# Query head 4 loaded early, with a ring of six slots for the first 18 gathers

## The chip, the cores and the metric

The kernel runs on one core of one Trainium2 chip. The time is the device time of one execution of the whole program, in microseconds (us); lower is better. The core has five engines with queues of their own (PE the matrix engine, DVE the vector engine, ACT the scalar engine, POOL for gathers and odd jobs, SP for plain transfers), 16 DMA engines that serve all queues, SBUF (on-chip memory, 128 partitions) and PSUM (matmul results, 8 banks). An engine executes its queue in order and waits on semaphores that others increment.

## The reference

One layer for 256 prompt tokens and 8 sample tokens, all float32, width 2048: a gated-linear-attention mixer and a short convolution in parallel, an output projection, and then a PEER block, which is where the change lies. Cut to that block:

```python
q = (ht @ w_query).reshape(T, 8, 2, 128)                   # 8 heads, two halves
s1, s2 = q[:, :, 0] @ sub_keys[0].T, q[:, :, 1] @ sub_keys[1].T   # 128 scores each
v1, i1 = top_k(s1, 16);  v2, i2 = top_k(s2, 16)
cand, cidx = v1[..., None] + v2[..., None, :], i1 * 128 + i2
top, pos = top_k(cand, 16);  idx = cidx[pos];  g = softmax(top)
u = expert_u[idx]                                          # gathered rows of 2048
w = g * gelu(einsum('thkd,td->thk', u, x))
out = einsum('thk,thkd->td', w, expert_v[idx])             # gathered rows again
```

Each token gathers 8 heads x 16 rows from expert_u and as many from expert_v, 8 KB each. The output is the normalised sum of the residual and this block, beside the new states.

## The kernel before, in words

**Stages.** Up to about 941 us the kernel projects: PE multiplies blocks of w_in and w_out, which SP loads into the four `raw` tiles, ACT copies to `w_hi` and DVE subtracts to `w_lo`. `mm_done` counts finished projection blocks and goes on counting through the query blocks: the 16 query blocks are numbered from `B_QRY`, two to a head (one per half), so head h is finished at `B_QRY + 2*h + 2`. Then the PEER block begins and lasts to the end.

**Gathers.** The PEER work is cut into 16 blocks g (8 heads for each of two tiles of 128 tokens) with 16 positions s each. For a position one gather brings 128 rows of expert_u (one for each token of the tile, 1 MB in all) and a later one 128 rows of expert_v. The list `order_of` sets their order: in the first block the U gathers of block 0 alone (gathers 0 to 15), from then on the U gather of block g and the V gather of block g-1 in turn, so that gather 16 is U of block 1, gather 17 is V of block 0 at s = 0, and so on; 16 more serve the sample tokens, 528 in all. POOL issues them in this order (`fetch`, L705), each into a ring slot of 8 KB a partition, and `free_slot` (L691) first waits until the gather that had the slot before was consumed. There are `RING = 8` slots, used as n % 8 (`slot_of`, L303). Two lie over `w_lo`, two over `w_hi`, three over `x_tok` (these wait until `x2_turned` says that PE has read it), one over `act_lo`.

**Consumers.** DVE's `dot` (L1450) multiplies a U gather with the tokens and frees its slot. After the sixteenth, ACT applies Gelu (L1029), DVE multiplies with the softmax weights (`weights_of`, L1476), and ACT makes diagonal matrices `diag` (L1040). The V gathers go half to PE, which adds diag x rows into PSUM (`weigh`, L1868), and half to DVE (`weigh`, L1466). Between these DVE runs the selection for the block after (keys_of, pairs_of, experts_of), which gives the indices `idx_all`.

**Query heads.** SP loads the weights of head h into `wq[h]` (16 KB a partition, 2 MB), which has three places, used as h % 3. Head 0 is computed in pieces around 941 us, heads 1 and 2 right behind it. The others are interleaved with the weighing of V rows, as `QUERIES = {1: (3, 4), 2: (5, 6), 3: (7,)}` says: in loop step b = 1 PE computes heads 3 and 4 in quarters between its V rows, and so on. ACT takes the results out (`query_head`, L974), and PE cannot begin the scores of a half, nor the next head but one half, before ACT has read the PSUM bank. `row_scale((1, 2), 2)` (L1556) turns the sums of squares of token tiles 1 and 2 into scales; it waits for a square root on ACT (L1024). `ROWS` says in which block DVE normalises these tiles (`row_tile`).

**What sets the order.** Each engine's instruction list is written out by hand in one block of code for each engine; the ring is the only place where POOL, DVE, PE and the DMA engines pace each other.

Of the kernel before, what the change touches and what calls it, by code (L numbers as in the profile page):

```python
# [17 lines left out]
F32 = mybir.dt.float32  # L18
# [6 lines left out]
P = 128  # L25
# [7 lines left out]
def hybrid_step(nc, x_prompt, x_sample, state_gla, state_conv, norm1_g, w_in, w_alpha_up, b_alpha,  # L33
                gla_norm_g, conv_w, conv_b, w_out, norm2_g, w_query, sub_keys, expert_u, expert_v,
                norm_f_g, y_prompt, y_sample, gla_prompt, conv_prompt, gla_sample, conv_sample):
    D = x_prompt.shape[2]
    TP, TS = x_prompt.shape[1], x_sample.shape[0]
    T = TP + TS
    KT = D // P
# [5 lines left out]
    PH, TOPK = 8, 16  # L45
# [15 lines left out]
    B_QRY = B_OUT + KT  # L61
# [27 lines left out]
    with ExitStack() as ctx:  # L89
        top = (nc.sbuf_base + 63) // 64 * 64  # L90
        where = [top]

        def sb_at(name, shape, dt, at):
            return nc.alloc_sbuf_tensor_at(name, shape, dt, offset=at)

        def room(nbytes):
            at = where[0]
            where[0] += (nbytes + 31) // 32 * 32
            assert where[0] <= nc.sbuf_usable_end, (where[0], nc.sbuf_usable_end)
            return at  # L100

        def size(shape):
            n = 4
            for s in shape[1:]:
                n *= s
            return n
# [4 lines left out]
        def sem(name):  # L111
            return ctx.enter_context(nc.semaphore(name))
# [19 lines left out]
        mean_b = sb("mean_b", [P, 1])  # L132
        keep = where[0]

        where[0] = (where[0] + 255) // 256 * 256
        at_act = where[0]
        act_hi = sb("act_hi", [P, KT, T], F32R)
        act_lo = sb("act_lo", [P, KT, T], F32R)
        at_raw = where[0]
        raw = [sb(f"raw{s}", [P, KT, P]) for s in range(4)]  # L140
        at_w = where[0]
# [3 lines left out]
        at_qk = room(4 * KT * T)  # L145
# [5 lines left out]
        at_tok = room(4 * 3 * D)  # L151
# [99 lines left out]
        diag_s = [sb(f"diag_s{s}", [P, TS]) for s in range(PH)]  # L251

        RING = 8
        ring_at = ([at_act + 3 * size([P, D])] + [at_w + s * size([P, D]) for s in (2, 3, 0, 1)]
                   + [at_tok + s * size([P, D]) for s in range(3)])
        ring = [sb_at(f"ring{s}", [P, D], F32, at) for s, at in enumerate(ring_at)]
        g_row = sb("g_row", [P, D])
        two = 2 * size([P, D])
        wq_at = (at_qk + size([P, D]), at_raw + two, at_raw)
        wq = [sb_at(f"wq{h}", [P, KT, 2 * P], F32, wq_at[h % 3]) for h in range(PH)]  # L260

        xs_rep = sb_at("xs_rep", [P, D], F32, at_h2T)
        gf_row = sb_at("gf_row", [P, D], F32, at_h2T + size([P, D]))
        y_tok = x2_tok

        S_U, S_V = 10, 12
        ROWS = 4
        QUERIES = {1: (3, 4), 2: (5, 6), 3: (7,)}

        def on_pe(g, s):  # L270

            return s % 2 == 0 if g < N_BLK - 1 else s in (0, 3, 6, 9, 12, 14)
# [12 lines left out]
        order_of = []  # L285
# [14 lines left out]

        diag_free = [done_at[n][1] for n, (kind, _, _, who) in enumerate(order_of) if kind == V_ and who == "pe"]

        slot_of = [n % RING for n in range(len(order_of))]  # L303
        before = [max((z for z in range(max(n - 2 * RING, 0), n) if slot_of[z] == slot_of[n]), default=None)
                  for n in range(len(order_of))]
        nth_in_slot = [slot_of[:n].count(slot_of[n]) for n in range(len(order_of))]
# [28 lines left out]
        mm_done = sem("mm_done")  # L335
# [139 lines left out]
        def _(sp):  # L475
# [63 lines left out]
            def load_query(h):  # L539

                sp.dma_start(wq[h][:], wqry[:, :, 2 * h * P:2 * (h + 1) * P]).then_inc(wq_in[h], 16)
# [3 lines left out]
            load_query(1)  # L545
            sp.wait_ge(lo_done, B_QRY)
            load_query(2)
            for h in range(3, PH):
                sp.wait_ge(mm_done, B_QRY + 2 * (h - 3) + 2)
                load_query(h)  # L550

            sp.wait_ge(mm_done, B_END)
# [18 lines left out]
        def _(pool):  # L571
            g = nc.gpsimd
            n = 0
# [117 lines left out]
            def free_slot(n):  # L691

                if before[n] is None:
                    if slot_of[n] in (5, 6, 7):
                        pool.wait_ge(x2_turned, 12)
                else:
                    who, count = done_at[before[n]]
                    if who == "dot":
                        pool.wait_ge(u_used, count)
                    elif who == "dve":  # L700
                        pool.wait_ge(dve_used, count)
                    else:
                        pool.wait_ge(pe_used, count)
# [26 lines left out]
        def _(act):  # L730
# [243 lines left out]
            def query_head(h):  # L974

                n0 = B_QRY + 2 * h
                query_out(n0)
                query_out(n0 + 1)
                scores_out(n0)
                scores_out(n0 + 1)  # L980
# [38 lines left out]
            scores_out(B_QRY + 1)  # L1019
            query_head(1)  # L1020
            soft_exp(1, P, rstd[:, 0:1])
            query_head(2)
            act.wait_ge(ms_done, 3)
            a.activation(root[:, 1:3], mean_sq[:, 1:3], ACT.Sqrt).then_inc(rt_done, 1)  # L1024
            n_soft = 2
            for b in range(1, N_BLK + 1):
                blk = slice((b - 1) * TOPK, b * TOPK)
# [19 lines left out]
                if b + 1 < N_BLK:  # L1047
                    soft_exp(n_soft, P, rstd[:, (b + 1) // PH:(b + 1) // PH + 1])
                    n_soft += 1
                for h in QUERIES.get(b, ()):  # L1050
                    query_head(h)
# [24 lines left out]
        def _(dve):  # L1076
# [496 lines left out]
            for b in range(N_BLK + 1):  # L1573
                for s in range(TOPK):
                    if b < N_BLK:
                        dot(b, s)
                    if b > 0:
                        if s == 0:
                            weights_of(b - 1)
                            if b == S_U + 1:  # L1580
                                dve.wait_ge(ws_gelu, 1)
                                v.tensor_tensor(w_s[:], w_s[:], g_s[:], ALU.mult).then_inc(ws_ready, 1)
                        if not on_pe(b - 1, s):
                            weigh(b - 1, s)
                    if b == S_U and s % 2:
                        dot_s(s // 2)
                    if b == 0:
                        if s == 2:
                            keys_of(1)
                        if s == 4:  # L1590
                            pairs_of(1)
                        if s == 6:
                            experts_of(1)
                        if s == 12:
                            row_scale((1, 2), 2)
                    elif b + 1 < N_BLK:
                        if s == 1:
                            keys_of(b + 1)
                        if s == 4:
                            pairs_of(b + 1)  # L1600
                        if s == 7:
                            experts_of(b + 1)
                    if b == ROWS and s in (9, 12):
                        if s == 9:
                            dve.wait_ge(mm_done, B_END)
                        row_tile(1 if s == 9 else 2)
                    if b == 7 and s in (9, 11, 13):
                        sample_step(s)
                    if b == 8 and s == 9:
                        sample_own()  # L1610
                    for t, at in ((0, 9), (2, S_V + 1)):
                        if b == at:
                            if s == 2:
                                y_add(t)
                            if s == 6:
                                y_mean_of(t)
                            if s == 9:
                                y_scale(t)
# [15 lines left out]
        def _(pe):  # L1634
# [334 lines left out]
                turn_rows(2, j)  # L1969
            for half in range(2):  # L1970
                rest_scores(half)
            for h in range(1, 3):
                for half in range(2):
                    query(B_QRY + 2 * h + half, every_k)
                for half in range(2):
                    scores(B_QRY + 2 * h + half)
# [3 lines left out]
            for b in range(1, N_BLK + 1):  # L1980
                for s in range(TOPK):
# [14 lines left out]
                    if b == S_V and s % 2:  # L1996
                        weigh_s(s // 2)
                        if s // 2 == PH - 1:
                            pe.wait_ge(pe_used, eaten(VS_, 0, PH - 1))
                            pe.sem_inc(sum_ready, 1)  # L2000
                    for m, h in enumerate(QUERIES.get(b, ())):
                        if s % 2 == 0 and 8 * m <= s < 8 * m + 8:
# [55 lines left out]
```

## Time and profile before

| | |
|---|---|
| median of 3 runs | 2312.95 us (2312.52 to 2313.0) |
| profiled execution | 2313.0 us, of which the span is 2311.3 us |
| TensorE clock granted, mean | 0.87 |
| busy: PE, DVE, POOL, ACT | 1789.2, 1602.8, 945.2, 597.6 us |
| gathers (software queue q0 in all) | 597.80 MB |
| plain loads and stores of SP (q1) | 179.97 MB |
| gather, from issue to landing, median | 14.0 us (U), 13.7 us (V) |
| load of one wq tile, from issue to landing, median | 25.8 us |

The span is what lies between the first and the last instruction; 1.7 us lie around it. A busy share over the whole span mixes two stages. Before 941 us PE is busy without a break and the DMA engines are not; afterwards the DMA engines are busy nearly all the time and no engine is. Tile names stand without their numbers, so `ring` is any slot.

### The profile page before, as it was taken

How to read it: one execution, taken by the hardware profiler on the slowest of the kernel's cores; microseconds unless marked ns; L12 is line 12 of the kernel's file. 1: busy time of each engine (PE TensorE's matmuls, PEld its weight loads, DVE VectorE, ACT ScalarE, POOL GpSimd, SP SyncE). 2: the span in 40 equal slices, each digit the busy share in tenths (PEclk: the TensorE clock that was granted, in tenths of full speed). 3: DMA queues.
4: the chain of work that ended last, by engine and by line, in shares of the span. 5: the costliest groups of instructions: out<-in, count | busy, mean ns of one | idle time of the engine just before them, and what ended most of it. 6: DMA issues, size and time to landing. Idle time of an engine off the chain costs nothing.

```text
span 2311.3 us, 24004 instructions
## 1 busy us (share of the span) xinstructions
PE 1789.2 (77%) x9239; PEld 1274.4 (55%) x9239; DVE 1602.8 (69%) x2035; ACT 597.6 (26%) x897; POOL 945.2 (41%) x736
## 2 busy tenths in 40 slices
PE   8999999999999999957786565666644456655565
PEld 8999999999999999834443222222211122122222
DVE  5544556646555554497787888889788887687766
ACT  5333555545545543410110000001000010010001
POOL 2000110110111101266575656557676665567653
PEclk9999999999999999979997767777677777877768
DMA  9866878887878776699999999999999999999997
GB/s 249 215 188 200 230 229 244 245 246 211 255 211 253 218 228 203 233 419 423 423 427 427 427 427 427 427 427 400 427 427 427 428 426 428 427 417 414 427 427 336
DMA packets 433958, 781.58 MB, mean 338 GB/s; under 512 B 39104, under 2 KB 353368, under 8 KB 365736
## 3 DMA queue, kind: packets, MB, share of 16 engines
q0 software_dynamic: 89424, 597.80, 62.1%
q1 hardware_dynamic: 342800, 179.97, 27.7%
q10 hardware_dynamic: 1624, 2.31, 0.3%
q8 instruction: 73, 1.20, 0.2%
q14 instruction: 37, 0.30, 0.0%
HBM read 756.74 MB, written 23.35 MB: 338 GB/s over the span
## 4 chain that ended last, share of the span: by engine, by line
PE 51%; DMA 31%; DVE 7%; POOL 7%; issue 3%; ACT 1%; DVEq 0%; SPq 0%; POOLq 0%; ACTq 0%
DMA ring<-in_expert_v,idx_all 27%; PE bank L1698 12%; PE bank L1699 12%; PE bank L1700 12%; PE bank L1875 10%; POOL ring L709 7%; DVE ring L1454 3%; DMA ring<-in_expert_u,idx_all 2%; DMA ring<-in_expert_v,idx_s 1%; DVE x_tok L1473 1%; PE bank L1810 1%; PE bank L1854 1%; PE bank L1791 1%; DMA ring<-in_expert_u,idx_s 1%; PE bank L1897 0%
## 5 line engine op out<-in xcount | busy, mean ns | idle before, releaser
L1875 PE MATMUL bank<-ring,diag 128*128 128x512 f32 x1008 | 680.7, 838 | 477.8 <-DMA ring<-in_expert_v,idx_all 392.8
L1875 PEld LDWEIGHTS bank<-ring,diag 128*128 128x128 f32 x1008 | 262.8, 273 | 884.5 <-issue 792.6
L1454 DVE CUSTOM_DVE_ANT_0 ring<-ring,xn_tok 128x2048 f32<-128x2048 f32 x256 | 583.6, 2289 | 220.2 <-DMA ring<-in_expert_u,idx_all 214.7
L1698 PE MATMUL bank<-act_hi,w_hi 128*128 128x264 f32 x2272 | 653.6, 288 | 2.4 <-DVE w_lo L1087 2.4
L1699 PE MATMUL bank<-act_lo,w_hi 128*128 128x264 f32 x2272 | 644.5, 284 | 0.0
L1700 PE MATMUL bank<-act_hi,w_lo 128*128 128x264 f32 x2272 | 644.1, 284 | 0.0
L1087 DVE TENSOR_TENSOR w_lo<-raw,w_hi 128x2048 fp32r<-128x2048 f32 x142 | 325.6, 2293 | 319.0 <-ACT w_hi L740 318.2
L709 POOL DMA_INDIRECT ring<-in_expert_u,idx_all x256 | 434.3, 1696 | 267.6 <-DVE w_all L1454 88.7
L709 POOL DMA_INDIRECT ring<-in_expert_v,idx_all x256 | 377.5, 1475 | 276.2 <-PE bank L1875 207.7
L1698 PEld LDWEIGHTS bank<-act_hi,w_hi 128*128 128x128 f32 x2272 | 428.6, 189 | 21.5 <-issue 18.6
L1699 PEld LDWEIGHTS bank<-act_lo,w_hi 128*128 128x128 f32 x2272 | 429.0, 189 | 1.7 <-issue 1.7
L1700 PEld LDWEIGHTS bank<-act_hi,w_lo 128*128 128x128 f32 x2272 | 426.7, 188 | 0.0
L740 ACT ACTIVATE w_hi<-raw 128x2048 fp32r<-128x2048 f32 x142 | 272.1, 1916 | 423.5 <-PE bank L1700 417.6
L1473 DVE SCALAR_TENSOR_TENSOR x_tok<-ring,w_all,x_tok 128x2048 f32<-128x2048 f32 (+1 forms) x130 | 305.2, 2348 | 31.7 <-DMA ring<-in_expert_v,idx_all 25.8
L663 POOL DMA_DIRECT2D out<-s_ring x64 | 35.0, 546 | 496.0 <-DVE s_ring L1305 496.0
L1029 ACT ACTIVATE w_all<-w_all 128x16 f32<-128x16 f32 x16 | 3.4, 216 | 626.6 <-DVE w_all L1454 626.6
L1854 PE MATMUL bank<-h2T,wq 128*128 128x264 f32 x448 | 103.3, 386 | 0.0
L1854 PEld LDWEIGHTS bank<-h2T,wq 128*128 128x128 f32 x448 | 85.0, 190 | 23.3 <-issue 10.2
L984 ACT ACTIVATE soft<-soft,rstd 128x16 f32<-128x16 f32 x16 | 4.9, 307 | 288.7 <-DVE soft L1397 288.7
L637 POOL DMA_DIRECT2D v_samples<-v_tok x1 | 0.8, 757 | 164.1 <-DVE v_tok L1213 164.1
L1897 PE MATMUL bank<-ring,diag_s 128*8 128x512 f32 x64 | 38.2, 754 | 24.4 <-DMA ring<-in_expert_v,idx_s 24.4
L1040 ACT ACTIVATE diag<-ident,w_all 128x128 f32<-128x128 f32 x127 | 38.8, 388 | 62.0 <-DVE w_all L1479 62.0
(299 smaller groups left out, 1139.5 us busy)
## 6 DMA issues: line engine op xcount, KB each, us to landing
raw<-in_w_in SPq DMA_DIRECT2D x129, 1024.0 KB, 6.7
s_ring<-in_state_gla POOLq DMA_DIRECT2D x64, 256.0 KB, 5.8
out<-s_ring POOLq DMA_DIRECT2D x64, 256.0 KB, 5.8
raw<-in_w_out SPq DMA_DIRECT2D x16, 1024.0 KB, 5.6
wq<-in_w_query SPq DMA_DIRECT2D x8, 2048.0 KB, 25.8
v_row<-v_samples POOLq DMA_DIRECT2D x32, 256.0 KB, 6.1
ring<-in_expert_u,idx_all POOLq DMA_INDIRECT x256, 14.0
ring<-in_expert_v,idx_all POOLq DMA_INDIRECT x256, 13.7
```

Of the source, the lines that this page charges most:

```text
L709: g.indirect_dma_start(ring[slot_of[n]][:], None, table, bass.IndirectOffsetOnAxis(ap=idx, axis=0)).then_inc(ring_in[slot_of[n]], 16)
L740: a.activation(w_hi[n0 % 2][:], raw[s][:], ACT.Copy).then_inc(hi_done, 1)
L1040: a.activation(diag[n_diag % N_DIAG][:], ident[:], ACT.Copy, scale=w_all[:, col:col + 1]).then_inc(diag_ready, 1)
L1087: v.tensor_tensor(w_lo[n0 % 2][:], raw[s][:], w_hi[n0 % 2][:].bitcast(F32), ALU.subtract).then_inc(lo_done, 1)
L1454: v.tensor_tensor_reduce(ring[k][:], ring[k][:], xn_tok[:, b // PH, :], 1.0, 0.0, ALU.mult, ALU.add, w_all[:, b * TOPK + s:b * TOPK + s + ...
L1473: v.scalar_tensor_tensor(out=y_tok[:, t, mine], in0=ring[k][:, mine], scalar=w_all[:, b * TOPK + s:b * TOPK + s + 1], in1=y_tok[:, t, mine ...
L1698: mm(out, hi_, act_hi[:, k, :], start=(k == 0), stop=False)
L1699: mm(out, hi_, act_lo[:, k, :], start=False, stop=False)
L1700: ins = mm(out, lo_, act_hi[:, k, :], start=False, stop=(k == KT - 1))
L1854: ins = mm(out, w[:, k, cols_], h2T[:, k, :], start=(k == 0), stop=(k == KT - 1))
L1875: ins = mm(bank[sum_bank(t) + j][:], diag[nth % N_DIAG][:], ring[k][:, j * 512:(j + 1) * 512], start=first, stop=stop)
L1897: ins = mm(bank[sum_bank(2) + j][0:TS, :], diag_s[s][:], ring[k][:, j * 512:(j + 1) * 512], start=(s == 0), stop=(s == PH - 1))
```

## The change

Six things are edited together.

- The start of `act_hi` is no longer rounded up to 256 bytes. It was at 20480 and is now at 20288, so all that is laid out behind it moves down by 192 bytes, and the ring slots and `raw` tiles now start 64 bytes past a multiple of 256.
- `wq[4]` gets a place of its own over the two `w_hi` tiles, and SP loads it as the fourth, as soon as the last projection is finished (`mm_done >= B_QRY`), before head 3. The waits of heads 5 to 7 are those of the places that they now take over.
- The two ring slots that lie there come last in the list (6 and 7). Gathers 0 to 17 use the first six slots alone, and the first use of slots 6 and 7, gathers 24 and 25, waits for PE to finish head 4 (`mm_done >= B_QRY + 10`).
- PE computes heads 3 and 4 ahead of all weighing, behind heads 1 and 2; ACT takes them out ahead of the Gelu of block 0. Heads 5, 6 and 7 move up to steps 1 and 2.
- The square root for tiles 1 and 2 moves on ACT ahead of head 2, and `row_scale` on DVE from s = 12 to s = 6 of step 0.
- `ROWS` goes from 4 to 3.

```diff
--- before.py
+++ after.py
@@ -132,7 +132,6 @@
         mean_b = sb("mean_b", [P, 1])
         keep = where[0]
 
-        where[0] = (where[0] + 255) // 256 * 256
         at_act = where[0]
         act_hi = sb("act_hi", [P, KT, T], F32R)
         act_lo = sb("act_lo", [P, KT, T], F32R)
@@ -251,21 +250,21 @@
         diag_s = [sb(f"diag_s{s}", [P, TS]) for s in range(PH)]
 
         RING = 8
-        ring_at = ([at_act + 3 * size([P, D])] + [at_w + s * size([P, D]) for s in (2, 3, 0, 1)]
-                   + [at_tok + s * size([P, D]) for s in range(3)])
+        ring_at = ([at_act + 3 * size([P, D]), at_w + 2 * size([P, D]), at_w + 3 * size([P, D])]
+                   + [at_tok + s * size([P, D]) for s in range(3)] + [at_w, at_w + size([P, D])])
         ring = [sb_at(f"ring{s}", [P, D], F32, at) for s, at in enumerate(ring_at)]
         g_row = sb("g_row", [P, D])
         two = 2 * size([P, D])
-        wq_at = (at_qk + size([P, D]), at_raw + two, at_raw)
-        wq = [sb_at(f"wq{h}", [P, KT, 2 * P], F32, wq_at[h % 3]) for h in range(PH)]
+        wq_at = (at_qk + size([P, D]), at_raw + two, at_raw, at_qk + size([P, D]), at_w, at_raw + two, at_raw, at_qk + size([P, D]))
+        wq = [sb_at(f"wq{h}", [P, KT, 2 * P], F32, at) for h, at in enumerate(wq_at)]
 
         xs_rep = sb_at("xs_rep", [P, D], F32, at_h2T)
         gf_row = sb_at("gf_row", [P, D], F32, at_h2T + size([P, D]))
         y_tok = x2_tok
 
         S_U, S_V = 10, 12
-        ROWS = 4
-        QUERIES = {1: (3, 4), 2: (5, 6), 3: (7,)}
+        ROWS = 3
+        QUERIES = {1: (5, 6), 2: (7,)}
 
         def on_pe(g, s):
 
@@ -300,7 +299,8 @@
 
         diag_free = [done_at[n][1] for n, (kind, _, _, who) in enumerate(order_of) if kind == V_ and who == "pe"]
 
-        slot_of = [n % RING for n in range(len(order_of))]
+        FEW = 6
+        slot_of = [n % FEW if n < 3 * FEW else (n - 3 * FEW) % RING for n in range(len(order_of))]
         before = [max((z for z in range(max(n - 2 * RING, 0), n) if slot_of[z] == slot_of[n]), default=None)
                   for n in range(len(order_of))]
         nth_in_slot = [slot_of[:n].count(slot_of[n]) for n in range(len(order_of))]
@@ -545,8 +545,12 @@
             load_query(1)
             sp.wait_ge(lo_done, B_QRY)
             load_query(2)
-            for h in range(3, PH):
-                sp.wait_ge(mm_done, B_QRY + 2 * (h - 3) + 2)
+            sp.wait_ge(mm_done, B_QRY)
+            load_query(4)
+            sp.wait_ge(mm_done, B_QRY + 2)
+            load_query(3)
+            for h in (5, 6, 7):
+                sp.wait_ge(mm_done, B_QRY + 2 * (h - 4) + 2)
                 load_query(h)
 
             sp.wait_ge(mm_done, B_END)
@@ -691,8 +695,10 @@
             def free_slot(n):
 
                 if before[n] is None:
-                    if slot_of[n] in (5, 6, 7):
+                    if slot_of[n] in (3, 4, 5):
                         pool.wait_ge(x2_turned, 12)
+                    if slot_of[n] >= FEW:
+                        pool.wait_ge(mm_done, B_QRY + 10)
                 else:
                     who, count = done_at[before[n]]
                     if who == "dot":
@@ -1019,9 +1025,10 @@
             scores_out(B_QRY + 1)
             query_head(1)
             soft_exp(1, P, rstd[:, 0:1])
-            query_head(2)
             act.wait_ge(ms_done, 3)
             a.activation(root[:, 1:3], mean_sq[:, 1:3], ACT.Sqrt).then_inc(rt_done, 1)
+            for h in (2, 3, 4):
+                query_head(h)
             n_soft = 2
             for b in range(1, N_BLK + 1):
                 blk = slice((b - 1) * TOPK, b * TOPK)
@@ -1591,7 +1598,6 @@
                             pairs_of(1)
                         if s == 6:
                             experts_of(1)
-                        if s == 12:
                             row_scale((1, 2), 2)
                     elif b + 1 < N_BLK:
                         if s == 1:
@@ -1969,7 +1975,7 @@
                 turn_rows(2, j)
             for half in range(2):
                 rest_scores(half)
-            for h in range(1, 3):
+            for h in range(1, 5):
                 for half in range(2):
                     query(B_QRY + 2 * h + half, every_k)
                 for half in range(2):
```

How PE's queue stands behind head 2, before. `wq_202` to `wq_204` are the weights of heads 2 to 4, `keysT` marks the scores of a head, `ring,diag` the weighing of one gather of V rows:

```order
L1854 MATMUL bank<-h2T,wq_202 128x264 x32
L1865 MATMUL bank<-keysT,stage_139 128x128 x2
L1865 MATMUL bank<-keysT,stage_138 128x128 x2
L1875 MATMUL bank<-ring_192,diag_175 128x512 x4
L1854 MATMUL bank<-h2T,wq_203 128x264 x8
L1875 MATMUL bank<-ring_196,diag_176 128x512 x4
L1854 MATMUL bank<-h2T,wq_203 128x264 x8
L1875 MATMUL bank<-ring_192,diag_177 128x512 x4
L1854 MATMUL bank<-h2T,wq_203 128x264 x8
```

And after the change:

```order
L1860 MATMUL bank<-h2T,wq_202 128x264 x32
L1871 MATMUL bank<-keysT,stage_139 128x128 x2
L1871 MATMUL bank<-keysT,stage_138 128x128 x2
L1860 MATMUL bank<-h2T,wq_203 128x264 x32
L1871 MATMUL bank<-keysT,stage_139 128x128 x2
L1871 MATMUL bank<-keysT,stage_138 128x128 x2
L1860 MATMUL bank<-h2T,wq_204 128x264 x32
L1871 MATMUL bank<-keysT,stage_139 128x128 x2
L1871 MATMUL bank<-keysT,stage_138 128x128 x2
L1881 MATMUL bank<-ring_196,diag_175 128x512 x4
L1860 MATMUL bank<-h2T,wq_205 128x264 x8
```

Two whole heads now stand between the scores of head 2 and the first weighing, which reads gather 17.

ACT's queue from the softmax of block 1 to the first diagonal matrices, before. `q_s` and `stage` take out a half head, `sc` its scores, `root` is the square root, `w_all` the Gelu:

```order
L984 ACTIVATE soft<-soft,rstd 128x16 [waits soft_in]
L962 ACTIVATE q_s<-bank 128x8 [waits mm_done]
L964 ACTIVATE stage_139<-bank 128x256
L962 ACTIVATE q_s<-bank 128x8 [waits mm_done]
L964 ACTIVATE stage_138<-bank 128x256
L971 ACTIVATE sc<-bank 128x2x128 [waits sc_mm] x2
L1024 ACT_TABLE_LOAD
L1024 ACTIVATE root<-mean_sq 128x2 [waits ms_done]
L1029 ACT_TABLE_LOAD
L1029 ACTIVATE w_all<-w_all 128x16 [waits u_used]
L1040 ACTIVATE diag_175<-ident,w_all 128x128 [waits w_ready]
```

After the change, the same stretch up to the outputs of head 2:

```order
L990 ACTIVATE soft<-soft,rstd 128x16 [waits soft_in]
L1029 ACT_TABLE_LOAD
L1029 ACTIVATE root<-mean_sq 128x2 [waits ms_done]
L968 ACTIVATE q_s<-bank 128x8 [waits mm_done]
L970 ACTIVATE stage_139<-bank 128x256
L968 ACTIVATE q_s<-bank 128x8 [waits mm_done]
L970 ACTIVATE stage_138<-bank 128x256
L977 ACTIVATE sc<-bank 128x2x128 [waits sc_mm] x2
```

The same five rows of output follow once more for head 3 and once for head 4, of which the last two are shown, and behind them:

```order
L970 ACTIVATE stage_138<-bank 128x256
L977 ACTIVATE sc<-bank 128x2x128 [waits sc_mm] x2
L1036 ACT_TABLE_LOAD
L1036 ACTIVATE w_all<-w_all 128x16 [waits u_used]
L1047 ACTIVATE diag_175<-ident,w_all 128x128 [waits w_ready]
L1047 ACTIVATE diag_176<-ident,w_all 128x128
```

The square root with its wait for DVE (`ms_done`) now stands ahead of head 2, and the Gelu behind the outputs of head 4.

POOL's queue from gather 16 on, before. `ring_191` to `ring_198` are slots 0 to 7, and the semaphore names who must have freed the slot:

```order
L709 DMA ring_191<-in_expert_u,idx_all 128x2048 [waits u_used,retrieved]
L709 DMA ring_192<-in_expert_v,idx_all 128x2048 [waits u_used]
L709 DMA ring_193<-in_expert_u,idx_all 128x2048 [waits u_used]
L709 DMA ring_194<-in_expert_v,idx_all 128x2048 [waits u_used]
L709 DMA ring_195<-in_expert_u,idx_all 128x2048 [waits u_used]
L709 DMA ring_196<-in_expert_v,idx_all 128x2048 [waits u_used]
L709 DMA ring_197<-in_expert_u,idx_all 128x2048 [waits u_used]
L709 DMA ring_198<-in_expert_v,idx_all 128x2048 [waits u_used]
L709 DMA ring_191<-in_expert_u,idx_all 128x2048 [waits u_used]
L709 DMA ring_192<-in_expert_v,idx_all 128x2048 [waits pe_used]
```

After:

```order
L715 DMA ring_195<-in_expert_u,idx_all 128x2048 [waits u_used,retrieved]
L715 DMA ring_196<-in_expert_v,idx_all 128x2048 [waits u_used]
L715 DMA ring_191<-in_expert_u,idx_all 128x2048 [waits u_used]
L715 DMA ring_192<-in_expert_v,idx_all 128x2048 [waits u_used]
L715 DMA ring_193<-in_expert_u,idx_all 128x2048 [waits u_used]
L715 DMA ring_194<-in_expert_v,idx_all 128x2048 [waits u_used]
L715 DMA ring_195<-in_expert_u,idx_all 128x2048 [waits u_used]
L715 DMA ring_196<-in_expert_v,idx_all 128x2048 [waits pe_used]
L715 DMA ring_197<-in_expert_u,idx_all 128x2048 [waits mm_done]
L715 DMA ring_198<-in_expert_v,idx_all 128x2048 [waits mm_done]
L715 DMA ring_191<-in_expert_u,idx_all 128x2048 [waits u_used]
```

The first gather that waits for PE's weighing (`pe_used`) is gather 25 before and gather 23 after, and everything behind it on POOL waits with it.

## Rows read from the trace of the kernel before

**Rows 1.** The page: busy tenths of the DMA engines in 40 slices of the span.
```profile
DMA  9866878887878776699999999999999999999997
```

**Rows 2.** Busy time by stretch, DMA share and GB/s last; the header names the columns.
```profile
core 0: us, PE busy (x) PEld busy (x) DVE busy (x) ACT busy (x) POOL busy (x), PEclk, DMA share, GB/s
...
943.00:959.00 16.00, 16.00 (x144) 16.00 (x143) 9.47 (x41) 8.16 (x20) 0.00 (x0) 1.00 0.01 2
...
1020.00:1030.00 10.00, 4.97 (x6) 2.18 (x7) 9.93 (x16) 3.95 (x10) 6.76 (x4) 0.51 1.02 419
```

**Rows 3.** DMA queues (packets, MB, share of 16 engines), stretch 955 to 1060.
```profile
q0 software_dynamic: 4880, 35.60, 80.3%
q1 hardware_dynamic: 6192, 6.29, 17.2%
```

**Rows 4.** DMA queues, stretch 955 to 1040.
```profile
q0 software_dynamic: 3704, 27.07, 75.5%
q1 hardware_dynamic: 6164, 6.27, 21.2%
```

**Rows 5.** DMA queues, stretch 1110 to 1145.
```profile
q0 software_dynamic: 1775, 12.92, 87.4%
q1 hardware_dynamic: 1775, 1.82, 14.6%
```

**Rows 6.** DMA queues, stretch 1150 to 1200.
```profile
q0 software_dynamic: 2928, 21.33, 101.0%
```

**Rows 7.** DMA queues, stretch 1229 to 1240 (q1 holds gf_row).
```profile
q1 hardware_dynamic: 144, 1.05, 22.6%
```

**Rows 8.** DMA queues, stretch 963 to 964.
```profile
q0 software_dynamic: 12, 0.10, 23.2%
```

**Rows 9.** PE in order of time (start us, us, line, tiles, count, [idle before]).
```profile
966.29 14.41 PE L1854 MATMUL bank<-h2T,wq 128*128 128x264 f32 x64
...
981.78 14.41 PE L1854 MATMUL bank<-h2T,wq 128*128 128x264 f32 x64
996.03 1.42 PE L1865 MATMUL bank<-keysT,stage 128*128 128x128 f32 x8
1025.03 6.10 PE L1875 MATMUL bank<-ring,diag 128*128 128x512 f32 x8 [27.58 <-ACT diag L1040]
...
1034.53 3.60 PE L1875 MATMUL bank<-ring,diag 128*128 128x512 f32 x8
...
1052.24 3.67 PE L1875 MATMUL bank<-ring,diag 128*128 128x512 f32 x8 [2.79 <-DMA ring<-in_expert_v,idx_all]
```

**Rows 10.** ACT in order of time.
```profile
997.48 0.38 ACT L971 ACTIVATE sc<-bank 128x256 f32<-128x256 f32 x1 [0.42 <-PE bank L1865]
997.88 1.28 ACT L1024 ACT_TABLE_LOAD   x1
1015.08 0.20 ACT L1024 ACTIVATE root<-mean_sq 128x2 f32<-128x2 f32 x1 [15.91 <-DVE mean_sq L1563]
...
1022.27 0.22 ACT L1029 ACTIVATE w_all<-w_all 128x16 f32<-128x16 f32 x1 [5.69 <-DVE w_all L1454]
...
1024.57 2.45 ACT L1040 ACTIVATE diag<-ident,w_all 128x128 f32<-128x128 f32 x8 [2.08 <-DVE w_all L1479]
```

**Rows 11.** DVE in order of time.
```profile
1001.24 2.29 DVE L1454 CUSTOM_DVE_ANT_0 ring<-ring,xn_tok 128x2048 f32<-128x2048 f32 x1
...
1014.51 0.33 DVE L1561 TENSOR_REDUCE ssq<-x_ss 128x1 f32<-128x4 f32 x2
...
1015.51 2.29 DVE L1454 CUSTOM_DVE_ANT_0 ring<-ring,xn_tok 128x2048 f32<-128x2048 f32 x1
...
1024.37 0.17 DVE L1479 TENSOR_TENSOR w_all<-w_all,g_all 128x16 f32<-128x16 f32 x1
```

**Rows 12.** POOL in order of time.
```profile
959.06 1.04 POOL L709 DMA_INDIRECT ring<-in_expert_u,idx_all  x1 [82.33 <-DVE idx_all L1440]
...
1031.40 0.94 POOL L709 DMA_INDIRECT ring<-in_expert_v,idx_all  x1 [3.73 <-PE bank L1875]
```


## The prediction

> **What bounds the kernel now.** I read the page's strip of DMA shares first [rows 1]: from slice 18 (about 980 us) on it stands at 9 to the end, where before it wanders between 6 and 8. The stretches confirm it. In 943 to 959 us, while PE is busy all 16 us, the DMA engines are idle (share 0.01) [rows 2]; from 960 us they are full, 419 GB/s in 1020 to 1030, although the clock of PE and the work of the others vary. In a clean stretch gathers alone move 21.33 MB in 50 us, 0.427 MB/us [rows 6]. The 528 gathers are 528 x 1.0486 = 554 MB, which at that rate is 1297 us, the length of the stage. So the end of the program is set by two numbers alone: how many bytes are left at some point near 1060 us, and whether the DMA engines ever run dry after 960 us. I price every edit in these. The second limit to keep in view is DVE, busy 9.93 of 10 us at 1020 to 1030 [rows 2]: in the first block it paces the gathers, and the loads of wq fill what it leaves free.
>
> **The early load of head 4: a gain.** Before, up to 1060 us, three wq tiles pass in the crowded stage (6.29 MB on q1) beside 35.60 MB of gathers [rows 3], and two more follow. Afterwards wq[4] goes as soon as the last projection is done, at about 941 us, into the idle stretch; wq[3] still waits for head 0. What a wq tile costs in the crowd: in 1110 to 1145 us gathers move 12.92 MB where 35 x 0.427 = 14.94 were possible, so 1.82 MB of wq displace 2.02 MB [rows 5], a factor 1.11. A tile of 2.10 MB costs 2.33 MB or 5.4 us. The edit gives 5.4 us if nothing runs dry. Both ends: 4.9 us (2.10 MB at 0.427) and 5.4; I take 5.4.
>
> **Heads 3 and 4 ahead of the weighing, with the root ahead of head 2: a stall.** I follow the chain in order of time.
> - DVE ends the selection of block 1 at 1001.24, where its next dot starts, and row_scale now comes right there. From its first row to the root on ACT it took 1015.08 - 1014.51 = 0.57 us [rows 10, 11]. So the root is at 1001.8, and only then does ACT take out head 2, whose matmuls ended before 996.03 [rows 9]. PE waits until then. Two outputs of 0.4 us and the scores later, head 3 starts at about 1003.3.
> - A head takes PE 981.78 - 966.29 = 15.5 us [rows 9] at the full clock. Heads 3 and 4 end, with their scores, near 1003.3 + 31.0 = 1034.3; PE has idled 6 us and may begin at 1.2 GHz, for which I add 0.7 us (bounds 0 and 3): 1035.0.
> - ACT then ends the last score copy, 1.8 us from the start of the scores as in 996.03 to 997.86 [rows 9, 10], of which 0.4 to 0.6 lie behind the 1035.0: 1035.5. The table load is now on the path, 1.28 us [rows 10] (before it was over long before the Gelu at 1022.27). Gelu 0.22, DVE's multiplication 0.2 [rows 11] and the first diagonal 0.46 (1024.57 to 1025.03): PE weighs gather 17 from 1037.7, where before it did from 1025.03.
> - That weighing took 6.1 us at the low clock in 1025.03, and 3.6 to 3.7 in 1034.53 and, after 2.79 us of idle, in 1052.24 [rows 9]. PE now comes warm from head 4, so I take 3.8 (bounds 3.6 and 6.1): slot 5 is free at 1041.5.
>
> The Trainium skill bears on one term. ACT's table load shows 1.28 us, and on the row no gap behind it. The Trainium skill (ScalarE: Activation LUTs, "What ACT_TABLE_LOAD costs") counts a drain on top and gives 2.66 us for a switch. By the page as an estimate the stall is 1.4 us longer and the forecast that much later; no row here has work queued ahead of such a load and waited for behind it, so the sum keeps the row.
>
> **What the stall does to the DMA engines.** With six slots, gather 23 takes the slot of gather 17, the first V row of PE; before it was gather 25 that waited for it (POOL at 1031.40, right behind the weighing that began at 1025.03) [rows 9, 12]. Gathers 0 to 22 wait for dots alone, the last of them (block 1, s = 0) ended at 1024.37 [rows 11] ahead of the wait for the Gelu. So the DMA engines get 23 gathers, 24.12 MB, and four wq tiles, 8.39 MB, together 32.5 MB, and then nothing until gather 23. Before they moved 27.07 + 6.27 = 33.3 MB up to 1040 [rows 4]. At 0.42 MB/us the supply is out 2 us earlier, at 1038. Gather 23 is issued at 1041.7. From issue to first bytes took from 959.06 to between 963 and 964, where q0 shows its first 12 packets [rows 8, 12], so 4.5 us: bytes flow again at 1046.2. By the slow ends (cold PE in head 3 and in the weighing, +2.3 each) it is 1050.8; by the quick ones, with no clock loss and 4.0 us to first bytes, 1044.8. I know of smaller lags that all point one way (outputs of head 3 between its halves, an issue that took 2 to 3 us when POOL had waited), and take 1047.5, in the middle.
>
> Left at 1060 us, against before: 35.60 MB of gathers minus the two wq tiles then still to come (2 x 2.33 = 4.66) is what before had put behind it; after has 24.12 + 0.427 x (1060 - 1047.5) = 29.46. The difference is 30.94 - 29.46 = 1.48 MB, 3.5 us longer. Read the other way: the DMA engines are dry for 9.5 us and 5.4 of these are paid by the early load; the 0.6 left between the two ways is the rounding of the supply. Ends: resumption at 1044.8 gives +0.8 us, at 1050.8 +6.8.
>
> **The other edits.** Six slots in the first block: two gathers fewer are in flight, while DVE waits for the scores of head 1, but wq[5] and wq[6] come into just this stretch (heads 1 and 2 end at 980.5 and 996.0 [rows 9]); I take nothing, bounds 0 and +1.5 us. Slots over x_tok from gather 3 on, not 5: at most 1.2 us of delay behind a wq load that fills the engines, nothing. row_scale six dots earlier: the same 1.0 us of DVE (1014.51 to 1015.51 [rows 11]), nothing. row_tile one block earlier and head 7 in step 2: DVE and PE have slack where gathers are alone on the DMA engines; bounds -0.5 and +0.5, taken as nothing. Places moved by 192 bytes: see the third rival; nothing.
>
> **Sum.** 2313.0 (profiled execution, 0.05 above the median of 2312.95) + 3.5 + 0.5 for the thin supply in the first block = 2317.0 us.
>
> **Rivals.**
> - *The stall doesn't reach the DMA engines: not slower.* The place is gather 23. If heads 3 and 4 are through by about 1028 (PE not held by the root, an ACT that reads out head 2 first), the weighing ends at 1034 and bytes flow at 1038, just as the supply ends: 2313.0 - 5.4 = 2307.6. It decides from a resumption before 1044.0, where 0.427 x (1060 - t) makes up the 6.82 MB and gain and hole are equal. For it speaks that PE is idle 27.58 us behind head 2 before [rows 9] and two heads need 31; against it the six us that PE waits for the root.
> - *DVE doesn't catch up.* DVE waits from 1024.4 to about 1037.3, 13 us, where it was busy 9.93 of 10 [rows 2]. If the next block stays paced by DVE, the lag is paid whole: 13 - 5.4 = +7.6, 2320.6; with the slow clock of PE 2323. For it: nothing was left of DVE in the first block. Against: the ring refills with five gathers at once when the slots come free, 12 us of work for the DMA engines.
> - *The shifted addresses cost transfer time.* If each row of 8 KB that starts 64 bytes past a multiple of 256 costs 64 bytes more, at 37.9 engine-us per MB (101.0% x 50 x 16 / 21.33 [rows 6]) that is 2.4 ns a row, 4224 rows an engine, +10 us: 2327. Against it: gf_row starts, by its address, 64 bytes past such a multiple already before, and its load took 22.6% x 11 x 16 = 39.8 engine-us for 1.05 MB, 37.9 per MB [rows 7], the same. The Trainium skill (DMA: Bandwidth & Descriptors, "How a descriptor splits into AXI transactions") says that a descriptor off a 256-byte boundary also pays for the bytes from the boundary below. By that rule the gathers would be longer; the trace disagrees for a load of this offset.
>
> **How the numbers follow.** A change within 0.2% (4.6 us) can't be told from none here. The stall as reckoned: 60%, spread over 2314 to 2320, some two fifths of it above 2317.6. No dry stretch or a short one: 17%, 2307.6 to 2312. DVE behind: 15%. Addresses: 4%. The rest, 4%, is a change that comes out as nothing. That makes faster 0.12, same 0.44, slower 0.44. The range goes from 2309, inside the first rival, to 2323, through the second.
>
> **What would show it.** In the profile after: a wq load in 943 to 955 us; PE idle some 6 us between head 2's matmuls and its scores, and busy with L1860 to about 1035; ACT's Gelu of block 0 near 1037, DVE idle ahead of it for 13 us; POOL waiting for PE at gather 23, and a hole in the DMA share between 1038 and 1048. No hole there, or a second one later, makes the prediction wrong; q0 time per MB above 37.9 engine-us would be the addresses.

## The result, and the profile after

The changed kernel takes 2331.99 us (median of 4 runs, 2331.17 to 2333.67) against 2312.73 us of the kernel before: +19.3 us, ratio 1.0085 with a 95% interval of 1.0067 to 1.0102. The forecast was 2317.0 us, +4.0, with a range up to 2323. The direction is right and the size is not. The runs below split the 19.3 us: the new order of the work costs 2.7 us where 4.0 were reckoned, and the shifted addresses, the rival with 4%, cost the other 16.6.

The page of the changed kernel, the same strip as [rows 1] and the rate below it, shows both:

```profile
DMA  9877878877788777899999999999999999999997
GB/s 243 208 199 196 240 230 235 245 238 229 235 235 250 215 216 209 304 348 417 421 422 421 421 422 421 421 422 396 421 422 422 422 421 422 421 412 408 422 421 329
```

The DMA engines are as full as before, but their plateau is 421 to 422 GB/s; before it was 427. A full share says nothing about this, since an engine that takes longer over the same packet is busy too. Here are the queues in a stretch in which only gathers run, 1300 to 1400 us (packets, MB, share of 16 engines), first of the kernel before:

```profile
q0 software_dynamic: 5865, 42.70, 101.1%
```

and then of the changed one:

```profile
q0 software_dynamic: 5785, 42.13, 101.2%
```

The same share moves 1.35% fewer bytes. Over the 554 MB of the stage that would be 554 / 0.4213 - 554 / 0.4270 = 17.6 us. In engine-us per MB it is 1.012 x 1600 / 42.13 = 38.4, against 37.9.

The stretches of the changed kernel, as [rows 2], with one more:

```profile
943.00:959.00 16.00, 16.00 (x144) 15.72 (x143) 10.63 (x43) 9.53 (x24) 1.09 (x2) 1.00 0.35 112
1020.00:1030.00 10.00, 10.00 (x48) 8.62 (x49) 3.08 (x4) 0.98 (x4) 4.63 (x3) 1.00 1.02 414
1040.00:1050.00 10.00, 10.00 (x27) 5.57 (x27) 9.83 (x22) 1.95 (x4) 3.85 (x3) 0.77 0.30 103
```

The early load fills a third of the once idle stretch (share 0.35, before 0.01), DVE falls from 9.93 to 3.08 busy, and the DMA engines run nearly dry in 1040 to 1050 (share 0.30), as forecast. The chain behind it, PE in order of time, answers to [rows 9]:

```profile
1000.94 2.08 PE L1871 MATMUL bank<-keysT,stage 128*128 128x128 f32 x8 [6.21 <-ACT stage L970]
1002.81 16.47 PE L1860 MATMUL bank<-h2T,wq 128*128 128x264 f32 x64
...
1034.61 1.42 PE L1871 MATMUL bank<-keysT,stage 128*128 128x128 f32 x8
1038.67 6.59 PE L1881 MATMUL bank<-ring,diag 128*128 128x512 f32 x8 [2.64 <-ACT diag L1047]
```

ACT, as [rows 10]:

```profile
1000.34 0.20 ACT L1029 ACTIVATE root<-mean_sq 128x2 f32<-128x2 f32 x1 [7.18 <-DVE mean_sq L1570]
...
1036.47 1.28 ACT L1036 ACT_TABLE_LOAD   x1
1037.76 0.22 ACT L1036 ACTIVATE w_all<-w_all 128x16 f32<-128x16 f32 x1
```

DVE, as [rows 11], and POOL, as [rows 12]:

```profile
1038.01 0.18 DVE L1486 TENSOR_TENSOR w_all<-w_all,g_all 128x16 f32<-128x16 f32 x1 [14.81 <-ACT w_all L1036]
```

```profile
1045.54 0.94 POOL L715 DMA_INDIRECT ring<-in_expert_v,idx_all  x1 [20.30 <-PE bank L1881]
```

PE idles 6.21 us for ACT, DVE 14.81 us for the Gelu, and POOL waits 20.30 us for the weighing of gather 17. The table load lies on the path and costs 1.28 us up to the start of the Gelu, with no gap: the 2.66 us of the Trainium skill (ScalarE: Activation LUTs, "What ACT_TABLE_LOAD costs") are not seen in this row. The row of the forecast could not show this, since ACT waited 15.91 us for DVE behind it [rows 10].

### The profile page after: what moved, and what is told of

Read it like the earlier page. It is cut to its first block, busy times and chain, and to the rows that moved or that the text cites. A ratio compares the mean times of both kernels' runs of the same rounds, so it can differ in the third digit from the quotient of the medians.

```text
span 2332.5 us, 24004 instructions
## 1 busy us (share of the span) xinstructions
PE 1796.0 (77%) x9239; PEld 1276.5 (55%) x9239; DVE 1603.5 (69%) x2035; ACT 597.4 (26%) x897; POOL 949.5 (41%) x736
## 4 chain that ended last, share of the span: by engine, by line
PE 51%; DMA 31%; POOL 8%; DVE 6%; issue 3%; ACT 1%; POOLq 0%; DVEq 0%; SPq 0%; ACTq 0%
DMA ring<-in_expert_v,idx_all 27%; PE bank L1704 12%; PE bank L1705 12%; PE bank L1706 12%; PE bank L1881 9%; POOL ring L715 8%; DMA ring<-in_expert_v,idx_s 2%; PE bank L1860 2%; DVE ring L1461 1%; DMA ring<-in_expert_u,idx_all 1%; DVE x_tok L1480 1%; PE bank L1816 1%; PE bank L1903 1%; PE bank L1797 1%; DMA x2T<-x_turned 0%
## 6 DMA issues: line engine op xcount, KB each, us to landing
wq<-in_w_query SPq DMA_DIRECT2D x8, 2048.0 KB, 16.6
```

## Experiments

The runs were timed in three groups, each beside the kernel before: e1_round_back, e2_round_off, e3_root_behind and off128 (median of the kernel before 2312.99 us), ring64, half64, off32 and off256 (2312.74 us), and e3_late_load, half64_other, one64 and six64 (2312.82 us). A difference is to the median of the same group, and a ratio stands with its 95% interval.

**Rounding back (e1_round_back).** The changed kernel with one line more:

```diff
+        where[0] = (where[0] + 255) // 256 * 256
         at_act = where[0]
```

> The changed kernel with the rounding to 256 bytes put back, nothing else. Theory A (the shifted addresses slow the gathers by 42.70 to 42.13 MB per 100 us, 1.35% of a stage of 1297 us, 17.5 us): 2332.0 - 17.5 = 2314.5 us, and clean stretches at 427 GB/s again. Theory S (the new order alone makes the loss, by dry DMA engines or a lag of DVE): it stays at 2330 to 2332.

Measured: 2315.70 us, +2.7, ratio 1.0014 (1.0005 to 1.0024). Theory S falls: one line of layout gives back 16.6 of the 19.3 us. What the order of the work costs is 2.7 us (1.2 to 5.5 by the interval). Its dry stretch is still there. It is shorter in this execution, since PE was faster behind its waits: head 3 took 14.89 us and not 16.47, the first weighing 5.40 and not 6.59:

```profile
1040.00:1050.00 10.00, 10.00 (x31) 5.97 (x30) 9.83 (x22) 0.66 (x1) 5.76 (x4) 0.92 0.54 185
```

**Rounding off (e2_round_off).** The kernel before without that line.

> The kernel before without the rounding, nothing else: all tiles from act_hi on lie 192 bytes lower, 64 bytes past a multiple of 256. Theory A: 2313 + 17.5 = 2330 us, with 421 to 422 GB/s in clean stretches of the gather stage. Theory S: 2313 us, no change.

Measured: 2334.07 us, +21.1, ratio 1.0093 (1.0076 to 1.0109). Its rate in 1300 to 1400 us is that of the changed kernel:

```profile
q0 software_dynamic: 5781, 42.10, 101.2%
```

The line alone makes the loss. In this kernel it is 4.5 us dearer than in the changed one (16.6), but the intervals overlap, and between the profiled executions the line costs 20.7 and 19.7 us; so this is no difference to explain. That 21.1 is more than the 17.6 reckoned from the clean stretch is another matter, taken up with ring64.

**Root behind head 2 (e3_root_behind).** On ACT, in the run with the rounding back:

```diff
+            query_head(2)
             act.wait_ge(ms_done, 3)
             a.activation(root[:, 1:3], mean_sq[:, 1:3], ACT.Sqrt).then_inc(rt_done, 1)
-            for h in (2, 3, 4):
+            for h in (3, 4):
                 query_head(h)
```

> The changed kernel with the rounding put back and the square root of tiles 1 and 2 on ACT behind head 2 instead of ahead of it. If the idle PE behind head 2 (6.2 us in the changed kernel) feeds the dry stretch of the DMA engines, gather 23 is issued some 7 us earlier, the dry stretch is 1 to 3 us instead of 8 to 10, and the time is 6 to 7 us under the run with the rounding alone: about 2308. If the dry stretch is set elsewhere: no difference to that run.

Measured: 2307.39 us, -5.6, ratio 0.9976 (0.9966 to 0.9986), and 8.3 us under the run with the rounding alone, more than the 6 to 7 expected. It beats both kernels. Its PE in order of time:

```profile
995.91 1.42 PE L1873 MATMUL bank<-keysT,stage 128*128 128x128 f32 x8
997.17 14.41 PE L1862 MATMUL bank<-h2T,wq 128*128 128x264 f32 x64
...
1030.96 6.68 PE L1883 MATMUL bank<-ring,diag 128*128 128x512 f32 x8 [2.64 <-ACT diag L1049]
```

and its stretch:

```profile
1040.00:1050.00 10.00, 9.06 (x32) 5.74 (x31) 8.50 (x12) 0.00 (x0) 8.47 (x6) 1.00 1.00 411
```

PE goes from head 2 to head 3 without a wait, the first weighing begins 7.7 us earlier than in the changed kernel, POOL issues gather 23 at 1037.91 us, and the stretch that ran dry is full (share 1.00). DVE still waits for the Gelu, 5.97 us; the DMA engines stay full through it, so it does not show in the time.

**The load of head 4 back in the crowd (e3_late_load).** The run above, with SP's order changed:

```diff
-            sp.wait_ge(mm_done, B_QRY)
-            load_query(4)
             sp.wait_ge(mm_done, B_QRY + 2)
             load_query(3)
+            load_query(4)
```

> The run with the root behind head 2, with wq[4] loaded behind wq[3], once head 0 is done, and no longer in the idle stretch. If the early load is the gain of that run (2.10 MB out of the crowd, 5.4 us): 2307.4 + 5.4 = 2312.8 us. If the gain comes from the order of heads and row_scale instead: 2307.4.

Measured: 2312.93 us, +0.1, ratio 1.0002 (0.9992 to 1.0011). The whole gain (5.6 us against the kernel before) goes with the early load; the difference between the two runs is 5.7 us, and the factor read from [rows 5] gave 5.4. The late load does not act by holding up PE: heads 3 and 4 follow head 2 without a wait (997.30 and 1012.80 us), and the share in 1040 to 1050 is 1.03. What this run keeps of the change (six slots, the order of heads, `row_scale` and `row_tile` earlier) comes to nothing that can be measured, as forecast. The idle stretch is idle again:

```profile
943.00:959.00 16.00, 16.00 (x144) 16.00 (x143) 9.45 (x41) 8.15 (x20) 0.00 (x0) 1.00 0.01 2
```

Its first weighing stands behind the same 2.64 us of idle as in the three runs above, and took only 3.70 us:

```profile
1031.10 3.70 PE L1882 MATMUL bank<-ring,diag 128*128 128x512 f32 x8 [2.64 <-ACT diag L1048]
```

**Which boundary (off128, off32, off256).** The kernel before, with bytes added behind the rounding, which move every tile from act_hi on:

```diff
         where[0] = (where[0] + 255) // 256 * 256
+        where[0] += 128        # in two other runs 32, 256
```

> The kernel before with 128 bytes added behind the rounding: every tile from act_hi on starts 128 bytes past a multiple of 256. If what counts is any start off a 256-byte multiple: 2330 us, as with 64. If the price is that of the bytes from the boundary below (4 instead of 2 beats of 32 bytes to a row of 256 beats): twice the price of 64, 2313 + 35 = 2348 scaled from the measured 17.5, or 2313 + 20 by beats. If 128 is aligned enough: 2313.

> The kernel before with 32 bytes added behind the rounding. If any start off a multiple of 256 costs the same: 2334 us, as 64 and 128 bytes gave. If the price goes with the distance to a finer boundary (64 bytes): more than 2334.

> The kernel before with 256 bytes added behind the rounding, a control: every tile moves, none leaves its multiple of 256. If the boundary counts: 2313. If any move of the layout costs: 2334.

Measured: 128 bytes 2334.56 us, +21.6 (1.0093, 1.0076 to 1.0110); 32 bytes 2337.82, +25.1 (1.0111, 1.0094 to 1.0128); 256 bytes 2313.22, +0.5 (1.0002, 0.9992 to 1.0012). A move that keeps the multiple of 256 is free; 64 and 128 bytes off cost the same within the intervals. 32 bytes off cost a little more: the intervals overlap, but its queue is slower in the clean stretch too (42.02 MB against 42.10 to 42.14). 192 bytes off was not tried. A price by the bytes from the boundary below, which doubles from 64 to 128, is out. In 1300 to 1400 us the queue moved, with 32, 128 and 256 bytes added:

```profile
q0 software_dynamic: 5771, 42.02, 101.2%
```

```profile
q0 software_dynamic: 5788, 42.14, 101.3%
```

```profile
q0 software_dynamic: 5868, 42.73, 101.1%
```

**Which tiles, and how many.** The kernel before with ring slots moved off the boundary, and in three of the runs (ring64, half64, six64) what has to make room, `xn_tok`, `same_j` and the first wq place, 64 bytes up; half64_other and one64 move ring slots alone. The lines of the ring in ring64:

```diff
-        ring_at = ([at_act + 3 * size([P, D])] + [at_w + s * size([P, D]) for s in (2, 3, 0, 1)]
-                   + [at_tok + s * size([P, D]) for s in range(3)])
+        ring_at = ([at_act + 3 * size([P, D]) + 64] + [at_w + 64 + s * size([P, D]) for s in (2, 3, 0, 1)]
+                   + [at_tok - 192 + s * size([P, D]) for s in range(3)])
```

> The kernel before, rounding kept, with only the eight ring slots moved to 64 bytes past a multiple of 256 (slot 0 and the four over w up by 64, the three over x_tok down by 192), and with them xn_tok, same_j and the first wq place up by 64, to make room. Every other tile stays. If the destination of the gathers is what costs: all of it, 2313 + 21 = 2334 us. If it is the other tiles (loads of stage one, what the engines read): 2313.

> As ring64, but only the four slots over w (1 to 4) are moved, so half of the gathers land off the boundary. If each gather pays for itself: half of ring64's loss, 2313 + 10 = 2323 us. If the price only comes when all traffic is off (a lone load off the boundary showed none in the trace of before): far less, under 2316. If one kind slows the other: more than half, over 2327.

> The other half of the ring: slot 0 up by 64 and slots 5 to 7 down by 192 bytes, the four over w in place. If what counts is how much of the traffic is off the boundary, not which tiles: as half64, 2318 us. If the slots over w are cheap and these are dear: the rest of ring64's loss, 2313 + 19 - 5 = 2327 us.

> The kernel before with slot 0 alone 64 bytes past a multiple of 256, one gather in eight. If the price rises faster than the share of such gathers: below 1 us, 2313. If each gather paid alike: 2313 + 19/8 = 2315.4 us.

> Six of the eight slots 64 bytes past a multiple of 256 (0, 1, 2, 5, 6, 7; slots 3 and 4 in place). In proportion to ring64: 2313 + 14 = 2327 us. If the price rises with the square of the share, as 5.3 us at a half and 18.9 at all suggest: 2313 + 0.56 x 18.9 = 2323.6 us.

| slots off the boundary | run | median, us | difference | ratio (95% interval) | q0 in 1300 to 1400, MB |
|---|---|---|---|---|---|
| 1 of 8 | one64 | 2313.10 | +0.3 | 1.0001 (0.9992 to 1.0011) | 42.67 |
| 4 of 8, over w | half64 | 2318.06 | +5.3 | 1.0023 (1.0013 to 1.0033) | 42.62 |
| 4 of 8, the others | half64_other | 2316.46 | +3.6 | 1.0017 (1.0007 to 1.0026) | 42.61 |
| 6 of 8 | six64 | 2324.01 | +11.2 | 1.0048 (1.0031 to 1.0065) | 42.36 |
| 8 of 8 | ring64 | 2331.65 | +18.9 | 1.0084 (1.0067 to 1.0101) | 42.13 |

The destination of the gathers is what costs: ring64 gives 18.9 of the 21.1 us, and half64_other, in which nothing but ring slots moved, is slower than the kernel before with an interval clear of 1. In which half of the ring the slots lie matters little, 5.3 against 3.6 with intervals that overlap; half64 also moved one wq place, and the other did not.

The other 2.2 us of e2_round_off lie, as far as the traces tell, where wq loads run beside the gathers. In 960 to 1160 us the kernel before moves 73.61 MB of gathers, ring64 72.63 and e2_round_off 71.53 (off128 the same), with 10.4 MB of other loads in each. Off the boundary there the loss is 1.3% while two of the three wq places stay on it, and 2.8% when all are off. So the wq loads, too, seem to pay; they were not moved by themselves.

And the price rises faster than the share of such gathers: one slot in eight costs nothing that can be measured, a half costs a fifth to a good quarter of the whole, three quarters 0.59 of it. A price with the square of the share, scaled to ring64, would be 0.3, 4.7 and 10.6 us and lies inside every interval; it was guessed from half64 and ring64, so only the other three put it to the test. A price in proportion would be 2.4, 9.5 and 14.2 us. At a half it is outside both intervals (up to 7.6 and 6.0 us). At one and at six slots the intervals just reach it (2.5 and 15.0 us), though all four executions of six64 lie between 2323.0 and 2324.9, below its 2327. The rate agrees: in proportion six64 would move 42.27 MB in the clean stretch, by the square 42.38.

It moved:

```profile
q0 software_dynamic: 5817, 42.36, 101.1%
```

## Why the prediction was wrong

**The step that failed** is the last of the other edits, "Places moved by 192 bytes: see the third rival; nothing", and in the rival the reading of [rows 7]. The row is true: the load of gf_row, 64 bytes past a multiple of 256, took 37.9 engine-us per MB, the same as the gathers on the boundary. But it was 1.05 MB between gathers that all lay on the boundary. one64 has one gather in eight off the boundary through the whole stage, and finds nothing that can be measured either. When all of the traffic lies off the boundary, the same rows take 38.4. The row was read as a price for a row of 8 KB, where it was one point of a curve that bends, and the point at its free end. The rival's own sum, +10 us for 64 more bytes a row, was also too small: the runs give 16.6 to 21.1 us.

The Trainium skill (DMA: Bandwidth & Descriptors, "How a descriptor splits into AXI transactions") states the rule that this rival used, and the forecast gave it little weight because of that row. The page speaks of bytes that are fetched; here it was the place written to that moved. The runs agree with it that starts off a multiple of 256 cost, and that 256 itself is the boundary (+256 bytes is free, +128 is not). They don't agree with a price by the bytes below the start: that would be twice as much at 128 as at 64 bytes, and was 21.6 against 21.1 us.

**The steps that held.**
- The early load: 5.4 us forecast, 5.7 measured by e3_late_load against e3_root_behind.
- The stall: PE held by the root until 1001.8 in the forecast; its scores began at 1000.94. Gelu forecast for 1036.8, measured 1037.76; weighing 1037.7 against 1038.67. The wait of DVE, forecast 13 us, was 14.81.
- The dry stretch, forecast from 1038 to 1047.5. In the changed kernel all queues move 0.01 MB in 1041 to 1044, nothing in 1044 to 1047, and 0.14 MB in 1047 to 1048. That its end agrees to 0.3 us is luck: the terms below were off both ways and cancelled.

**Terms that were mis-sized.** Two are PE's clock. For the start of head 3 behind the idle PE 0.7 us were added; against heads at the full clock head 3 and the scores before it took 2.7 us more in the changed kernel (16.47 + 2.08 against 14.41 + 1.42), and 1.1 with the rounding back. The first weighing was taken as warm, 3.8 us; it took 6.59 us in the changed kernel (granted clock 0.56) and 5.40 with the rounding back (0.68). PE had idled only 2.64 us, less than the 2.79 of the row in [rows 9] that was fast, and e3_late_load was fast behind the same 2.64 (3.70 us, clock 1.00). The clock can't be told from the length of the idle time alone.

This made gather 23 later (1045.54 instead of 1041.7, 1043.04 with the rounding back), and yet the order costs 2.7 us, not more than the 4.0. Another term went the other way. The 4.5 us from issue to first bytes were read at the first gather of all [rows 12, rows 8], but there the engines were still full of a wq load: in 961 to 963 us q1 alone has a share of 103.7%. Onto idle engines the first bytes came 1.6 us behind the issue, in the changed kernel (1047.2) and with the rounding back (1044.6). In the latter q0 then moves 0.73 MB up to 1047, as if it had run at the full rate from 1045.3, so the term was too long by some 2 us. The 1.3 us added for lags (from 1046.2 to 1047.5) don't show either.

The balance at 1060 us bears this out, with the rounding back and in the manner of [rows 3]:

```profile
q0 software_dynamic: 4124, 30.12, 70.4%
q1 hardware_dynamic: 8256, 8.39, 23.0%
```

30.12 MB of gathers stand against 30.94 in the forecast's reckoning of before (35.60 less the two loads still to come): 0.82 MB, 1.9 us. The forecast had 29.46, 3.5 us. The interval of the 2.7 us (1.2 to 5.5) holds both, so the sum for the order came out right within what can be told, partly by terms that cancelled. The 0.5 us for a thin supply in the first block stays open; it is smaller than what these runs tell apart.

**The rivals.** That DVE doesn't catch up is out: with a wait of 14.81 us in the changed kernel the order costs 2.7 us, and with the rounding back the gathers move 42.73 MB in 1300 to 1400 us, the rate of before. The first rival, no dry stretch, names the right place: taking PE's wait away gives 2307.39 us, where it had 2307.6. Its condition was not met in the changed kernel, only in e3_root_behind.

## What to carry to other kernels

Where the DMA engines bound a stage, keep the tiles that take the bulk of the traffic on multiples of 256 bytes. Look at GB/s or time per MB there, not at the busy share: both kernels show 9 tenths, and one moves 1.35% less. A row that shows a cheap exception within other traffic tells the price of that exception, and not what the same offset costs when all the traffic has it. Before such a row is used to strike out a rival, ask how the price goes with the share, and widen the range to the rival's time. A delay read from a row holds for what else ran at that moment: the 4.5 us were read on full engines and used for idle ones. In an order written by hand, ask of each wait what stands behind it on its engine: one square root put ahead of one head cost 8.3 us.

## What the runs showed of the hardware

- Gathers of rows of 8 KB onto starts that are 32, 64 or 128 bytes past a multiple of 256 in SBUF run at 42.02, 42.10 and 42.14 MB per 100 us with all engines full, against 42.70 to 42.73 on the boundary. In the time of the program this is 25.1, 21.1 and 21.6 us, of tiles that were all moved together.
- The price depends on how much of the traffic is off the boundary, about as the square of the share (0.3, 3.6 to 5.3, 11.2, 18.9 us for 1, 4, 6, 8 of 8 slots). Why it bends was not found. That neighbouring transfers get in each other's way would fit, but no run measured it.
- PE's clock after 2.6 to 2.8 us of idle was low in some runs and not in others: behind 2.64 us of idle the eight matmuls of a weighing took 6.59, 5.40, 6.68 and 3.70 us at a granted clock of 0.56, 0.68, 0.55 and 1.00 (after, e1_round_back, e3_root_behind, e3_late_load), and 3.67 us at 1.00 behind 2.79 us in [rows 9]. What decides between them was not found.
- From the issue of a gather to its first bytes it took 1.6 us with the DMA engines idle (after and e1_round_back), and 4 to 5 us behind a wq load that filled them [rows 8, 12].
